# The first two weight units behind two RMS norms, run block by block together

## The chip, the cores and the metric

The kernel runs on one NeuronCore of a Trainium2 chip. The metric is the device time of one execution in microseconds (us). The profile comes from one execution taken by the hardware profiler. TensorE (PE in the rows, PEld its weight loads) multiplies matrices, VectorE (DVE), ScalarE (ACT) and GpSimd (POOL) work elementwise, SyncE (SP) issues most transfers. TensorE's clock has two levels, 1.2 and 2.4 GHz; the rows give the granted clock as a share of full speed, 0.50 or 1.00.

## What is computed

Two transformer blocks on 512 tokens of width 1024, in float32. The first has 16 meta tokens ahead of the sequence, a token mixer (a state space model and an mLSTM) and a gated FFN; the second has a mixed attention and an MLP. Both sublayers of the first block add a normed result, and their sum is normed again for what follows:

```python
def rmsnorm(x, g):
    return x * rsqrt(mean(x * x, -1) + 1e-6) * g
# token_mixer:    x1 = x + rmsnorm(merged @ w_out, g_mix_post)
# channel_mixer:  h = rmsnorm(x1, g_ffn_pre)
#                 y = (gelu(conv3(h @ w_gate)) * (h @ w_up)) @ w_down     (2816 wide)
#                 x2 = x1 + rmsnorm(y, g_ffn_post)
# second block:   q, k, v, ... = rms_norm(x2, attn_norm) @ w_in
```

The change lies at the two places where such a pair of norms stands: x1 to the FFN, and x2 to the second block's projections.

## The kernel before

Activations lie transposed, features in the 128 partitions and tokens along the free axis, as eight tiles (KT = 8) of 128 features. Weights come in 227 units of 128 x 1024 float32, in a ring of four buffers. A unit is one tile of 128 output features: eight blocks of 128 x 128, one for each tile of the input. Every operand is split in a high and a low part of a faster type, and each block takes three products, high by high, low by high and high by low. ScalarE makes w_hi (`split_hi`, L348) and VectorE w_lo (`split_lo`, L848), each two units ahead (LOOK = 2).

On TensorE `unit` (L1689) issues the 24 products of a unit (48 where the output is 516 columns, in two halves of 258), `begin` (L1706) waits first for the unit's w_lo and for the evacuation of the unit before the last, whose PSUM banks it takes over. Each engine works through its own list in a fixed order, and semaphores tie the lists together.

**The stretch around a post norm.** The sublayer's last units leave y_sum. Its squares are summed over the features by products with a matrix of ones (`column_sums`, L1723, plain float32). `rstd` (L868) makes rs of the sums: a scaling on VectorE, a reciprocal root on ScalarE, three Newton steps on VectorE. Then VectorE's `residual` (L1218) goes through the eight tiles: scale y_sum by rs, add it to x (`x1_ready` or `x2_ready`), and, once ScalarE has made h_hi of the tile, make h_lo (`h2_lo` or `h3_lo`). ScalarE also squares the tile (`tile_square`, L369) for the next norm. TensorE does not wait for the next norm's rs: the units run on x times the gain alone, and rs is multiplied in when a unit is evacuated. So the first unit behind the norm (`ffn_gate` of U_FFN, or `wide(U_V2, ...)`) waits block by block for h_lo, and behind each block stands `tile_sum` (L1733), the column sums of that tile's squares. When all eight are through (`stat_mm`), VectorE's second `rstd` makes the new rs, and the first unit is evacuated with it (gate_pad, or v2T), then the second. The third unit needs the first one's banks.

Behind the first norm a gate unit (516 columns, banks 0 and 1 or 2 and 3) and an up unit (512 columns) alternate, and GpSimd convolves the gate's result. Behind the second norm come eight units of values (`wide`, 512 columns, banks 0 and 1 in turn). Each is evacuated to v2T, turned by four transposes on TensorE (`v2_transposes`, L1991, banks 2 and 3 in turn) and copied by ScalarE (`v2_copy`, L654), in a list where the copy of unit n - 1 stands in front of the split of unit n + 3.

Of the kernel before, what the change touches and what calls it, by code (L numbers as in the profile page):

```python
# [23 lines left out]
P = 128  # L24
D_MODEL = 1024
KT = D_MODEL // P
SEQ, META = 512, 16
T1 = SEQ + META
HALF = T1 // 2
T0 = 12  # L30
TW = T1 - T0
# [14 lines left out]
RING = 4  # L46
# [18 lines left out]
U_FFN = U_OUT + KT  # L65
FFN_CHUNKS = (8, 8, 6)
U_V2 = U_FFN + 2 * FFN_TILES + 3 * KT
U_F2 = U_V2 + KT
U_G0 = U_F2 + 1
U_QK2 = U_G0 + 1  # L70
# [74 lines left out]
def build(nc, w_units, x_t, cols_in, consts_in, sel_in, ssm_b_in, ssm_c_in, alibi_in, dil_in, out):  # L145
# [6 lines left out]
    def fixed(name, shape, dt=fp32):  # L152
        t = nc.alloc_sbuf_tensor_at(name, [P] + shape, dt, offset=place[0])
        place[0] += (4 * math.prod(shape) + 31) // 32 * 32
        return t
# [10 lines left out]
    whi = fixed("w_hi", [RING, 1024], f32r)  # L166
    wlo = fixed("w_lo", [RING, 1024], f32r)
    tile528 = KT * T1 * 4
    Zx = region(tile528)
    hhi = fixed("h_hi", [KT, T1], f32r)  # L170
    hlo = fixed("h_lo", [KT, T1], f32r)
# [86 lines left out]
    PS = nc.alloc_psum_tensor("ps", [P, 8, 512], fp32)  # L258
# [3 lines left out]
    def sem(name):  # L262
        if name not in sems:
            sems[name] = nc.alloc_semaphore(name)
        return sems[name]
# [3 lines left out]
    unit_done, evacuated = sem("unit_done"), sem("evacuated")  # L269
# [38 lines left out]
    with block as block:  # L308
# [1377 lines left out]
        def _(pe):  # L1686
            mm = nc.tensor.matmul

            def unit(s, r, xhi, xlo, outs, ready=None, base=0, blocks=None, last_of_unit=True, after=None):  # L1689


                blocks = blocks or [(k, k) for k in range(KT)]
                for b, (kw, kx) in enumerate(blocks):
                    if ready is not None:
                        pe.wait_ge(ready, base + kx + 1)
                    w = slice(kw * P, kw * P + P)
                    for a, (wt, xt) in enumerate(((whi, xhi), (whi, xlo), (wlo, xhi))):
                        for o, c0, n in outs:
                            ins = mm(o, wt[:, s % RING, w], xt[:, kx, c0:c0 + n], start=(b == 0 and a == 0),  # L1699
                                     stop=(b == len(blocks) - 1 and a == 2))  # L1700
                    if last_of_unit and b == len(blocks) - 1:
                        ins.then_inc(unit_done, 1)
                    if after is not None:
                        after(b)

            def begin(s, r=0):  # L1706
                pe.wait_ge(lo_ready, r + (s + 1))
                if s >= 2:
                    pe.wait_ge(evacuated, r + (s - 1))
# [5 lines left out]
            def late_halves(s, b0=None, c0=T0):  # L1715
                b = 2 * (s % 2) if b0 is None else b0
                return [(PS[:, b + h, 0:TH], c0 + TH * h, TH) for h in range(2)]

            def column_sums(n, src, start, stop):

                outs = [(4, 0, n // 2), (5, n // 2, n // 2)] if n != SEQ else [(4, 0, SEQ)]
                for b, c0, k in outs:
                    ins = mm(PS[:, b, 0:k], ones, src[:, c0:c0 + k], start=start, stop=stop)  # L1723
                return ins
# [8 lines left out]
            def tile_sum(norm, n, m):  # L1733

                pe.wait_ge(sem("tile_sq"), KT * PRE.index(norm) + m + 1)
                column_sums(n, sqm[m] if norm == 5 else sq[m % 2], m == 0, m == KT - 1).then_inc(sem("tile_summed" if m < KT - 1 else "stat_mm"), 1)
# [156 lines left out]
            for n in range(U_GLU):  # L1893
                begin(n)
                if n == 0:
                    unit(n, 0, hhi, hlo, halves(n), sem("h1_lo"), after=lambda b: tile_sum(0, T1, b))
                else:
                    unit(n, 0, hhi, hlo, halves(n) if n < U_O else late_halves(n))
                if 1 <= n <= CT:
                    turn_tokens(n - 1)  # L1900
                if n in B_AFTER:
                    b_transposes(B_AFTER.index(n))
                if n == GATE_AFTER:
                    gate_transposes()
                if n == K_AFTER:
                    ssm_kernel()
                if n in Y_AFTER:
                    ssm_out(Y_AFTER.index(n))
                if n in E_AFTER:
                    ssm_in(E_AFTER.index(n))  # L1910
                if n in VT_AFTER:
                    v_transposes(VT_AFTER.index(n))
                if n >= U_GA - 1:
                    h, k = divmod(n - (U_GA - 1), 4)
                    if h < HEADS1:
                        (mlstm_broadcast, mlstm_scores, mlstm_values, mlstm_norm)[k](h)
# [5 lines left out]
            for n in range(U_GLU, U_MERGE):  # L1922
                begin(n)
                unit(n, 0, yahi, yalo, late_halves(n), None, 0, [(k, k) for k in range(4)], False)
                unit(n, 0, yahi, yalo, late_halves(n, 4 + 2 * (n % 2)), None, 0, [(4 + k, k) for k in range(4)])
# [9 lines left out]
            for s in (U_MERGE, U_MERGE + 1):  # L1935
                begin(s)
                branch(s, 1)
# [18 lines left out]

            def ffn_gate(s, r):
                begin(s, r)
                if isinstance(r, int) and s == U_FFN:
                    unit(s, r, hhi, hlo, late_halves(s, c0=0), sem("h2_lo"), after=lambda b: tile_sum(2, TW, b))  # L1960
                else:
                    unit(s, r, hhi, hlo, late_halves(s, c0=0))

            def ffn_up(s, r):
                begin(s, r)
                unit(s, r, hhi, hlo, [(PS[:, 2 * (s % 2), :], META - T0, SEQ)])

            def down(s, r, xhi, xlo, o, ready=None, base=0, tiles=KT):
                begin(s, r)
                unit(s, r, xhi, xlo, [(o, 0, SEQ)], ready, base, [(k, k) for k in range(tiles)])  # L1970

            s0, f0 = U_FFN, 0
            for c, tiles in enumerate(FFN_CHUNKS):
                for q in range(2):
                    ffn_gate(s0 + 2 * q, 0)
                    ffn_up(s0 + 2 * q + 1, 0)
                with pe.Fori(0, tiles // 2 - 1) as i:
                    for q in range(2, 4):
                        ffn_gate(s0 + 2 * q, i * 4)
                        ffn_up(s0 + 2 * q + 1, i * 4)  # L1980
                s0 += 2 * tiles
                with pe.Fori(0, 2) as i:
                    for j in range(4):
                        down(s0 + j, i * 4, fahi, falo, PS[:, 2 * ((s0 + j) % 2), :], sem("fa_lo") if j == 0 else None,
                             f0, tiles)
                f0 += tiles
                s0 += KT
# [3 lines left out]
            def v2_transposes(j):  # L1991
                pe.wait_ge(evacuated, U_V2 + j + 1)
                if j >= 2:
                    pe.wait_ge(sem("v2_ready"), j - 1)
                for t in range(4):
                    ins = nc.tensor.transpose(PS[:, 2 + j % 2, P * t:P * t + P], vT2[j % 2][:, P * t:P * t + P], ident)
                ins.then_inc(sem("v2t_mm"), 1)

            def wide(s, r=0, ready=None, norm=None):
                begin(s, r)  # L2000
                unit(s, r, hhi, hlo, [(PS[:, s % 2, :], 0, SEQ)], ready,
                     after=(lambda b: tile_sum(norm, SEQ, b)) if norm else None)

            pe.wait_ge(evacuated, U_V2)
            wide(U_V2, 0, sem("h3_lo"), 4)
            for n in range(U_V2 + 1, U_QK2):
                wide(n)
                if n <= U_F2:
                    v2_transposes(n - 1 - U_V2)

# [140 lines left out]
            for j in range(KT // 2):  # L2151
                s = U_OB + j
# [8 lines left out]
            for m in range(KT):  # L2161
                s = U_MLP + KT + m
                down(s, 0, mahi, malo, PS[:, s % 2, :], sem("ma_lo") if m == 0 else None, 0)
            with pe.Fori(0, 2) as c:
                for f in range(KT):
                    wide(U_MLP + 2 * KT + f, c * 16)
                for m in range(KT):
                    s = U_MLP + 3 * KT + m
# [3 lines left out]
            for m in range(KT):  # L2172
                s = U_MLP + 7 * KT + m
# [124 lines left out]
```

## Time and profile before

| | |
|---|---|
| median of 3 runs | 1564.51 us (1563.32 to 1565.14) |
| the profiled execution | 1565.74 us |
| its span, first to last instruction | 1563.9 us |
| busy: TensorE / its weight loads | 1496.9 us (96%) / 1290.1 us (82%) |
| busy: VectorE / ScalarE / GpSimd | 844.1 us (54%) / 616.3 us (39%) / 267.0 us (17%) |
| mean granted clock of TensorE | 0.986 |
| chain that ended last | TensorE 85%, VectorE 7%, GpSimd 4%, ScalarE 2%, issue 2% |

A busy TensorE need not be at its full rate: products are pipelined and the end of a record is modelled. The pitch from one record's start to the next is what a product costs in a row of them. The two stretches that the change touches are at about 442 to 490 us (first post norm) and 838 to 890 us (second).

### The profile page before, as it was taken

The numbers are of one execution on the slowest core, as the hardware profiler recorded it, in microseconds if no ns is written. First come the engines' busy times: TensorE is split into PE (matmuls) and PEld (weight loads), VectorE is DVE, ScalarE is ACT, GpSimd is POOL, SyncE is SP. The second block draws the span as 40 slices with busy tenths as digits, with TensorE's granted clock in tenths as the row PEclk, the third lists the DMA queues.
The fourth block names the chain that finished last, engine by engine and source line by source line (L and its number), as shares of the span: only waits on it lengthen the run. The fifth ranks groups of instructions, "written<-read, shape, count | busy, mean of one in ns | idle before, by whom it ended". The sixth has DMA issues, their size and how long they took to land.

```text
span 1563.9 us, 23462 instructions
## 1 busy us (share of the span) xinstructions
PE 1496.9 (96%) x9229; PEld 1290.1 (82%) x9229; DVE 844.1 (54%) x1227; ACT 616.3 (39%) x920; POOL 267.0 (17%) x272
## 2 busy tenths in 40 slices
PE   7978999999979999999997999999999999999998
PEld 7977999999968988988885777888886888888887
DVE  5779744357465543553455546776845533434344
ACT  5547655643243221231233334646534323223230
POOL 2664100000025613540632000000100000000000
PEclk9989999999999999999998999999999999999999
DMA  5211211123302222222232221111122222223221
GB/s 191 83 42 54 69 54 56 67 82 137 108 28 95 94 94 94 91 97 95 81 108 74 73 76 55 43 39 55 41 81 95 91 97 95 95 94 95 92 95 67
DMA packets 36006, 128.03 MB, mean 82 GB/s; under 512 B 4460, under 2 KB 4588, under 8 KB 35792
## 3 DMA queue, kind: packets, MB, share of 16 engines
q1 hardware_dynamic: 34464, 122.18, 23.3%
q10 hardware_dynamic: 864, 4.33, 0.7%
q8 instruction: 63, 1.03, 0.3%
q0 software_dynamic: 592, 0.30, 0.1%
q14 instruction: 23, 0.19, 0.0%
HBM read 124.68 MB, written 2.10 MB: 81 GB/s over the span
## 4 chain that ended last, share of the span: by engine, by line
PE 85%; DVE 7%; POOL 4%; ACT 2%; issue 2%; DMA 0%; SPq 0%; DVEq 0%; POOLq 0%; ACTq 0%
PE ps L1699 72%; PE ps L2036 2%; PE ps L2060 2%; PE ps L1881 1%; PE ps L1723 1%; POOL phase_tmp L1568 1%; PE ps L2047 1%; PE ps L1831 1%; DVE h_lo L866 1%; DVE w_lo L853 1%; PE ps L2014 1%; DVE x L866 1%; POOL acc L1568 1%; POOL phase L1568 1%; POOL conv_tmp L1657 1%
## 5 line engine op out<-in xcount | busy, mean ns | idle before, releaser
L1699 PE MATMUL ps<-h_hi,w_hi 128*128 128x258 f32 (+2 forms) x1768 | 512.3, 339 | 38.9 <-DVE h_lo L866 18.2
L1699 PE MATMUL ps<-h_lo,w_hi 128*128 128x258 f32 (+2 forms) x1768 | 494.3, 329 | 0.0
L1699 PE MATMUL ps<-h_hi,w_lo 128*128 128x258 f32 (+2 forms) x1768 | 493.2, 328 | 0.0
L853 DVE TENSOR_TENSOR w_lo<-w_raw,w_hi 128x1024 fp32r<-128x1024 f32 (+2 forms) x227 | 290.5, 1280 | 182.6 <-ACT w_hi L355 181.4
L1699 PEld LDWEIGHTS ps<-h_hi,w_hi 128*128 128x128 f32 x1768 | 301.9, 190 | 90.1 <-issue 34.8
L1699 PEld LDWEIGHTS ps<-h_lo,w_hi 128*128 128x128 f32 x1768 | 299.5, 190 | 33.8 <-issue 5.9
L1699 PEld LDWEIGHTS ps<-h_hi,w_lo 128*128 128x128 f32 x1768 | 299.5, 190 | 30.8
L355 ACT ACTIVATE w_hi<-w_raw 128x1024 fp32r<-128x1024 f32 (+2 forms) x227 | 233.2, 1035 | 199.6 <-PE ps L1699 198.6
L1699 PE MATMUL ps<-mlp_lo,w_hi 128*128 128x512 f32 x256 | 100.9, 394 | 0.0
L1699 PE MATMUL ps<-mlp_hi,w_hi 128*128 128x512 f32 x256 | 100.3, 392 | 0.0
L1699 PE MATMUL ps<-mlp_hi,w_lo 128*128 128x512 f32 x256 | 99.4, 388 | 0.0
L857 DVE TENSOR_TENSOR y_sum<-y_sum,ps 128x512 f32<-128x512 f32 (+1 forms) x40 | 27.5, 688 | 112.9 <-PE ps L1699 112.9
L1699 PE MATMUL ps<-ffn_hi,w_hi 128*128 128x512 f32 x176 | 68.7, 391 | 2.1 <-DVE ffn_lo L857 2.1
L1699 PE MATMUL ps<-ffn_hi,w_lo 128*128 128x512 f32 x176 | 69.3, 394 | 0.0
L1699 PE MATMUL ps<-ffn_lo,w_hi 128*128 128x512 f32 x176 | 68.9, 392 | 0.0
L1654 POOL TENSOR_SCALAR gate_conv<-gate_pad,cols 128x512 f32<-128x512 f32 x22 | 29.2, 1326 | 212.8 <-DVE gate_pad L857 212.8
L818 ACT ACTIVATE relu<-ps 128x512 f32<-128x512 f32 x32 | 19.2, 601 | 105.3 <-PE ps L1699 105.3
L626 ACT ACTIVATE gate_conv<-gate_conv 128x512 f32<-128x512 f32 x22 | 13.9, 632 | 117.3 <-POOL gate_conv L1568 117.3
L866 DVE SCALAR_TENSOR_TENSOR relu_sq<-ps,relu 128x512 f32<-128x512 f32 x32 | 22.1, 692 | 70.1 <-ACT relu L818 70.1
L1568 POOL TENSOR_TENSOR gate_conv<-gate_conv,conv_tmp 128x512 f32<-128x512 f32 x44 | 56.8, 1292 | 3.7
L1657 POOL TENSOR_SCALAR conv_tmp<-gate_pad,cols 128x512 f32<-128x512 f32 x44 | 56.7, 1289 | 4.2
L1699 PEld LDWEIGHTS ps<-mlp_hi,w_hi 128*128 128x128 f32 x256 | 48.1, 188 | 11.2
(292 smaller groups left out, 1936.3 us busy)
## 6 DMA issues: line engine op xcount, KB each, us to landing
w_raw<-w_units SPq DMA_DIRECT2D x227, 512.0 KB, 3.3
x<-x_t ACTq DMA_DIRECT2D x1, 2112.0 KB, 7.8
out<-out_tile SPq DMA_DIRECT2D x8, 256.0 KB, 2.0
x<-x_t ACTq DMA_DIRECT2D x3, 528.0 KB, 9.2
x<-x_t ACTq DMA_DIRECT2D x2, 264.0 KB, 4.7
consts<-consts SPq DMA_DIRECT2D x1, 320.0 KB, 6.9
b_step<-ssm_b SPq DMA_DIRECT2D x1, 256.0 KB, 10.4
c_step<-ssm_c SPq DMA_DIRECT2D x1, 256.0 KB, 11.3
```

Of the source, the lines that this page charges most:

```text
L355: A.do(dn.activation(whi[:, s % RING, 0:w], raw[:, s % RING, 0:w], ACT.Copy), hi_ready)
L818: A.do(dn.activation(rl[p][:, :], PS[:, s % 2, :], ACT.Relu), sem("relu_ready"))
L853: Dv.do(v.tensor_tensor(wlo[:, s % RING, 0:w], raw[:, s % RING, 0:w], f32(whi[:, s % RING, 0:w]), ALU.subtract), lo_ready)
L857: Dv.do(v.tensor_tensor(o, a, b, op), s)
L866: Dv.do(v.scalar_tensor_tensor(out=o, in0=a, scalar=sc, in1=b, op0=op0, op1=op1), s)
L1568: Po.do(g.tensor_tensor(o, a, b, op), s)
L1654: Po.do(g.tensor_scalar(dst[:, :], src[:, META:META + SEQ], w[0], w[3], M, A_))
L1657: Po.do(g.tensor_scalar(ctmp[:, :], src[:, META + k:META + k + SEQ], w[k], 0.0, M, A_))
L1699: ins = mm(o, wt[:, s % RING, w], xt[:, kx, c0:c0 + n], start=(b == 0 and a == 0), stop=(b == len(blocks) - 1 and a == 2))
L1723: ins = mm(PS[:, b, 0:k], ones, src[:, c0:c0 + k], start=start, stop=stop)
L2036: ins = mm(PS[:, b + bank, c:c + w], q[0:65, hh, P * t:P * t + P], k[0:65, hh, 0:w], start=False, stop=True, skip_group_check=True)
L2060: ins = mm(PS[:, 2 + 3 * hh, HD * t:HD * t + HD], Pb[hh][:, bank, c + P * k:c + P * k + P], V[:, k, HD * h:HD * h + HD], start=(k == 0), s ...
```

## The change

A new helper, `two_units`, runs two units over the same input together: it waits for block k of h_lo, issues block k of the first unit, then the column sums of tile k, then block k of the second unit (with `lag` = 0, as both calls have it). Behind the first post norm the pair is the first gate and the first up unit; behind the second it is the first two value units. The second unit's own `begin` moves between the first unit's first block and its own. The first value unit's transposes, which stood behind the second unit, now stand behind the third, directly ahead of the second unit's. Which products are computed does not change, nor does any other engine's list.

```diff
--- before.py
+++ after.py
@@ -1703,6 +1703,31 @@
                     if after is not None:
                         after(b)
 
+            def block_of(s, xhi, xlo, outs, k):
+
+                for a, (wt, xt) in enumerate(((whi, xhi), (whi, xlo), (wlo, xhi))):
+                    for o, c0, n in outs:
+                        ins = mm(o, wt[:, s % RING, k * P:k * P + P], xt[:, k, c0:c0 + n], start=(k == 0 and a == 0),
+                                 stop=(k == KT - 1 and a == 2))
+                return ins
+
+            def two_units(s, outs, ready, base, lag, after):
+
+                begin(s)
+                for k in range(KT + lag):
+                    if k < KT:
+                        pe.wait_ge(ready, base + k + 1)
+                        ins = block_of(s, hhi, hlo, outs[0], k)
+                        if k == KT - 1:
+                            ins.then_inc(unit_done, 1)
+                        after(k)
+                    if k == lag:
+                        begin(s + 1)
+                    if k >= lag:
+                        ins = block_of(s + 1, hhi, hlo, outs[1], k - lag)
+                        if k - lag == KT - 1:
+                            ins.then_inc(unit_done, 1)
+
             def begin(s, r=0):
                 pe.wait_ge(lo_ready, r + (s + 1))
                 if s >= 2:
@@ -1956,10 +1981,7 @@
 
             def ffn_gate(s, r):
                 begin(s, r)
-                if isinstance(r, int) and s == U_FFN:
-                    unit(s, r, hhi, hlo, late_halves(s, c0=0), sem("h2_lo"), after=lambda b: tile_sum(2, TW, b))
-                else:
-                    unit(s, r, hhi, hlo, late_halves(s, c0=0))
+                unit(s, r, hhi, hlo, late_halves(s, c0=0))
 
             def ffn_up(s, r):
                 begin(s, r)
@@ -1972,6 +1994,10 @@
             s0, f0 = U_FFN, 0
             for c, tiles in enumerate(FFN_CHUNKS):
                 for q in range(2):
+                    if s0 + 2 * q == U_FFN:
+                        two_units(U_FFN, (late_halves(U_FFN, c0=0), [(PS[:, 2 * ((U_FFN + 1) % 2), :], META - T0, SEQ)]), sem("h2_lo"), 0, 0,
+                                  lambda k: tile_sum(2, TW, k))
+                        continue
                     ffn_gate(s0 + 2 * q, 0)
                     ffn_up(s0 + 2 * q + 1, 0)
                 with pe.Fori(0, tiles // 2 - 1) as i:
@@ -2002,9 +2028,12 @@
                      after=(lambda b: tile_sum(norm, SEQ, b)) if norm else None)
 
             pe.wait_ge(evacuated, U_V2)
-            wide(U_V2, 0, sem("h3_lo"), 4)
-            for n in range(U_V2 + 1, U_QK2):
+            two_units(U_V2, [[(PS[:, (U_V2 + j) % 2, :], 0, SEQ)] for j in range(2)], sem("h3_lo"), 0, 0,
+                      lambda k: tile_sum(4, SEQ, k))
+            for n in range(U_V2 + 2, U_QK2):
                 wide(n)
+                if n == U_V2 + 2:
+                    v2_transposes(0)
                 if n <= U_F2:
                     v2_transposes(n - 1 - U_V2)
 
```

## Rows read from the trace of the kernel before

**Rows 1.** Page, chain that ended last; list of waits (total, times, longest).

```profile
PE 85%; DVE 7%; POOL 4%; ACT 2%; issue 2%; DMA 0%; SPq 0%; DVEq 0%; POOLq 0%; ACTq 0%
...
PE ps L1699 <- DVE h_lo L866: 18.2, 12, 6.9
```

**Rows 2.** Timeline, VectorE, first norm: start us, us, engine, line, operation.

```profile
465.20 0.76 DVE L866 SCALAR_TENSOR_TENSOR h_lo<-x,cols,h_hi 128x516 fp32r<-128x516 f32 x1 [0.18 <-ACT h_hi L608]
...
467.54 0.75 DVE L866 SCALAR_TENSOR_TENSOR h_lo<-x,cols,h_hi 128x516 fp32r<-128x516 f32 x1 [0.79 <-ACT h_hi L608]
...
469.01 1.23 DVE L853 TENSOR_TENSOR w_lo<-w_raw,w_hi 128x1024 fp32r<-128x1024 f32 x1 [0.72 <-ACT w_hi L355]
...
470.35 0.70 DVE L863 TENSOR_SCALAR rs<-ps 128x516 f32<-128x516 f32 x1
...
473.93 0.69 DVE L857 TENSOR_TENSOR gate_pad<-ps,rs 128x516 f32<-128x516 f32 x1
```

**Rows 3.** Timeline, TensorE, first norm.

```profile
452.04 0.77 PE L1699 MATMUL ps<-h_hi,w_hi 128*128 128x258 f32 x2 [6.86 <-DVE h_lo L866]
...
453.47 1.92 PE L1723 MATMUL ps<-sq,consts 128*128 128x258 f32 x4
...
468.35 0.51 PE L1699 MATMUL ps<-h_hi,w_hi 128*128 128x258 f32 x2 [0.48 <-DVE h_lo L866]
...
469.17 1.03 PE L1723 MATMUL ps<-sq,consts 128*128 128x258 f32 x4
...
469.85 0.58 PE L1699 MATMUL ps<-h_hi,w_hi 128*128 128x512 f32 x1
...
475.61 0.40 PE L1699 MATMUL ps<-h_hi,w_hi 128*128 128x258 f32 x2
```

**Rows 4.** Timeline, VectorE and TensorE, second norm.

```profile
852.38 0.77 PE L1699 MATMUL ps<-h_hi,w_hi 128*128 128x512 f32 x1 [6.77 <-DVE h_lo L866]
...
865.46 0.75 DVE L866 SCALAR_TENSOR_TENSOR h_lo<-x,cols,h_hi 128x512 fp32r<-128x512 f32 x1 [0.19 <-ACT h_hi L650]
...
867.79 0.75 DVE L866 SCALAR_TENSOR_TENSOR h_lo<-x,cols,h_hi 128x512 fp32r<-128x512 f32 x1 [0.79 <-ACT h_hi L650]
...
868.59 0.50 PE L1699 MATMUL ps<-h_hi,w_hi 128*128 128x512 f32 x1 [0.50 <-DVE h_lo L866]
...
869.39 1.02 PE L1723 MATMUL ps<-sq,consts 128*128 128x512 f32 x2
...
870.58 0.69 DVE L863 TENSOR_SCALAR rs<-ps 128x512 f32<-128x512 f32 x1
...
874.15 0.69 DVE L857 TENSOR_TENSOR v2T<-ps,rs 128x512 f32<-128x512 f32 x1
...
875.82 0.60 PE L1996 MATMUL ps<-consts,v2T 128*128 128x128 f32 x4
...
876.17 0.48 PE L1699 MATMUL ps<-h_hi,w_hi 128*128 128x512 f32 x1
```

**Rows 5.** Timeline, VectorE and TensorE, what follows behind each norm.

```profile
483.54 0.69 DVE L857 TENSOR_TENSOR gate_pad<-ps,rs 128x516 f32<-128x516 f32 x1
...
487.00 0.40 PE L1699 MATMUL ps<-h_hi,w_hi 128*128 128x258 f32 x2
...
878.03 1.23 DVE L853 TENSOR_TENSOR w_lo<-w_raw,w_hi 128x1024 fp32r<-128x1024 f32 x1 [1.32 <-ACT w_hi L355]
```

**Rows 6.** Windows: stretch, us, busy of five engines, granted clock, DMA share, GB/s.

```profile
124.85:128.70 3.85, 0.00 (x0) 0.00 (x0) 3.75 (x9) 3.69 (x6) 1.29 (x2) 1.00 0.00 0
...
128.70:136.70 8.00, 7.95 (x124) 7.78 (x125) 7.86 (x16) 5.87 (x8) 2.88 (x3) 0.79 0.07 22
...
452.00:460.00 8.00, 7.96 (x37) 7.24 (x38) 7.32 (x11) 3.99 (x7) 0.00 (x0) 0.71 0.01 2
...
852.00:860.00 8.00, 7.35 (x18) 4.37 (x19) 7.29 (x12) 3.73 (x6) 0.00 (x0) 0.75 0.00 0
...
929.50:936.50 7.00, 5.76 (x25) 4.54 (x25) 3.22 (x5) 1.58 (x2) 0.00 (x0) 1.00 0.20 74
```

## The prediction

> **What bounds the kernel now.** I read the chain's shares and the list of waits first [rows 1]. The chain that ended last is 85% TensorE: nearly everywhere the time is the number of matmuls times their pitch, so a change of order can only win where TensorE stands still or runs slowly. The wait for h_lo is the largest entry of TensorE's list, 18.2 us, and much of it lies behind the two post norms. There the profiled timeline shows the same picture twice. VectorE makes one block of the new h_lo every 2.34 us behind the first norm [rows 2] and every 2.33 us behind the second [rows 4], and TensorE has, for each block, only the products of the first unit and the column sums. After the eighth block comes the second unit, all at once, and beside it the chain that the third unit needs: scale the sums into rs, reciprocal root on ScalarE, three Newton steps, then the evacuation of the first unit. That chain starts at 470.35 and its evacuation ends at 473.93 + 0.69 = 474.62, which is 4.27 us [rows 2]; behind the second norm it runs from 870.58 to 874.15 + 0.69 = 874.84, 4.26 us [rows 4]. Today the second unit (5.6 us) covers it: the third unit starts without a wait, at 475.61 and at about 876.26 [rows 3, 4]. So the question is whether TensorE has room for the second unit's products between the blocks, and what covers the rs chain once the second unit is gone from behind it.
>
> **The prices, at full clock.** One block of the first FFN unit, six products of 258 columns, starts at 468.35 + 0.51 - 0.40 = 468.46 (a first record is longer by the time it waits at the array) and the sums start at 469.17: 0.71 us [rows 3]. The sums: the next unit's first product is recorded at 469.85 for 0.58 us where such a product takes 0.39, so it really streams from 470.04: the sums hold TensorE for 0.87 us. The whole second unit, 24 products of 512 columns, goes from 470.04 to 475.61, 5.57 us, or 0.70 us for the three products of a block [rows 3]. At the low clock I take double the last two; the first is seen: 452.04 + 0.77 - 0.63 = 452.18 to 453.47, 1.29 us [rows 3].
>
> **First norm, does TensorE keep up?** A block now asks of TensorE 0.71 + 0.87 + 0.70 = 2.28 us, against 2.34 us that VectorE gives. There is room, but only 0.06 us a block, and it starts with a debt. TensorE begins this stretch at 1.2 GHz: of 452 to 460 the granted clock is 0.71 on average, which is 0.29 x 2 x 8 = 4.6 us at half speed, until 456.6 [rows 6]. The first block's work takes 1.29 + 1.74 + 1.40 = 4.4 us there; the second starts at 456.6, when its h_lo has long been ready, is then at full clock, and ends at about 458.9. Five more blocks of 2.28 us put the start of the eighth at 470.3, where it is 468.46 today: 1.8 us late. This is worked out, not seen. Its sums end 0.71 + 0.87 + 0.17 us later (0.17 is what the drain adds: 469.17 + 1.03 - 470.04), at 472.05, and rs can begin at 472.1 instead of 470.35, where it waits for about the same time for the weight split in front of it. The evacuation then ends at 474.62 + 1.7 = 476.3, and the third unit streams from 476.45 instead of 475.61: **+0.85 us**. The second unit's seven blocks (4.9 us) did move into the gaps, but 1.8 us of that is lateness and the rest is a new wait: TensorE has finished block eight of both units at 470.3 + 2.3 = 472.6 and stands still until 476.45, **3.9 us**.
>
> **Second norm.** Same sum. Per block 0.70 + 0.87 + 0.70 = 2.27 us at most; the three products here are 0.69 and I use 2.25, against 2.33. Start 852.38 + 0.77 - 0.63 = 852.5 [rows 4]; the low clock lasts to 856.0 (0.25 x 2 x 8 = 4.0 us of 852 to 860) [rows 6], so the first block ends at 856.45, and six more of 2.25 us bring the eighth to 869.95; today it begins 0.16 us behind the end of h_lo at 868.54, so 1.25 us late [rows 4]. Today the sums end at 869.39 + 1.02 = 870.41, later 871.65; rs moves from 870.58 to 871.7, the evacuation ends at 875.95 and the third unit streams from 876.1. Today it streams from 876.17 + 0.48 - 0.39 = 876.26, but with the first transposes already done. These are moved behind it, four of them in 0.45 us (875.82 to 876.26) [rows 4], and must still be paid: **+0.3 us**. Here too the wait is 876.1 - 872.2 = **3.9 us**.
>
> **What the moved transposes stand in front of.** ScalarE's queue is copy, then the split of a later weight unit; the copy of the first transposes now waits for the third unit, and the split behind it with it. Today the split on VectorE ends at 878.03 + 1.23 = 879.26, 3.0 us behind the transposes [rows 5]; add an evacuation of 0.69 us, and 3.7 us have to fit beside the second transposes and the fourth unit, 0.45 + 5.57 = 6.0 us. They do: nothing, with 2.3 us in hand. Behind the first norm the whole FFN pipeline on GpSimd, ScalarE and VectorE starts 1.7 us later against a third unit that is 0.85 us later. Its next result TensorE asks for is the evacuation at 483.54 + 0.69 = 484.23, needed at 487.00 [rows 5]: 2.8 us in hand, no cost, and 0.9 us less in hand than today. No DMA is moved, GpSimd's and SP's queues keep their order, and no computation is added or dropped.
>
> **The clock.** What does TensorE do after a wait of 3.9 us? Nearly the same thing is in this trace. From 124.85 to 128.70 it stands still for 3.85 us with the clock at full, and of the next 8 us the granted clock is 0.79: 0.21 x 2 x 8 = 3.4 us at 1.2 GHz, with TensorE busy throughout [rows 6]. Two other waits, of 3.6 and of 3.1 us, have this same average behind them. A wait of 1.2 us, at 929.8 to 931.0, leaves the clock at 1.00 [rows 6]. The new waits are as long as the longest of these, so I expect the drop at both. Each costs half of 3.4 us, 1.7 us of work, **+3.4 us** for both; seen from the two stretches behind the norms it can be up to 4.6 us at the low clock (2.3 us each), and from the 1.2 us wait nothing. I take the middle value, since its wait is as long. The Trainium skill says, in TensorE: Matmul & The Clock Gate, "What's actually happening", that "the default state is throttled, and activity releases the throttle", and in "HAM oscillation — how this bites in real kernels" that every stall long enough starts the next burst cold, each time anew. That speaks against this change: the matmuls gathered into the gaps are paid back behind a stall. The rows agree for 3.85 us. With that rule the sum is +4.5 us, without it +1.1 us.
>
> **The sum.** 0.85 + 0.3 + 3.4 = 4.5 us. The profiled execution took 1565.74 us (span 1563.9 and 1.8 around it) and would take 1570.2. It lies 1.2 us above the median of the runs, 1564.51, which becomes 1569.0.
>
> **Rivals.** *The clock stays up* at one or both waits, since the wait is shared between two stretches of activity: +1.1 to +2.8 us, 1565.6 to 1567.3. For it speaks only the 1.2 us wait; against it the three long ones. Chance 0.18. *TensorE keeps pace* and the clock drops: if the first block costs less at the low clock than I make it, or blocks are done faster than 2.28 us, rs starts as today and the third units begin at 474.75 (-0.85 us) and 874.97 plus the transposes (-0.85 us); with the drops -1.7 + 3.4 = +1.7 us, 1566.2. Chance 0.10. *The other side:* it keeps pace and no drop comes: -1.7 us, 1562.8. It hangs on one thing, a block's work on TensorE against VectorE's 2.34 us: once the debt at block two is under 0.4 us (six blocks of 0.06) it is gone by block eight. Chance 0.05. More than this can't be won, since the rs chain of 4.3 us bounds the start of the third unit; over 3.1 us faster would need a gain that I don't see, 0.03. *More low stretches* than two, or a low clock over two such stretches, since all later work is shifted: 1571 or more, 0.04. The forecast itself, late blocks and two drops, has 0.60, and its own range is 1567.0 to 1571.0: the drops cost 1.5 to 2.3 us each, and a later rise of the clock in the first blocks adds its half to the lateness.
>
> **How the numbers follow.** A measurement here tells about 0.2%, 3.1 us, from no change. Slower by more: of the 0.60 some 0.52, with the last rival and the top of the first 0.60. Faster by more: 0.04. Within: 0.36. The range 1564.0 to 1571.2 leaves out the case of the other side, the unexplained gain, and most of the last, some 0.15.
>
> **What would show it.** In the changed profile, first norm: three products of 512 columns between the sums and the next block; the eighth block 1 to 2 us behind its h_lo; a wait of TensorE for gate_pad (behind the second norm for v2T) of 3.5 to 4 us; the granted clock at 0.5 for about 3.4 us behind each. The step on pace is wrong if the eighth block starts with its h_lo; the step on the clock if the third units run at the 0.23 us pitch from the first product. The forecast falls if the rs chain is no longer what the third unit waits for.

## The result and the profile after

| | before | changed |
|---|---|---|
| median | 1564.58 us | 1567.85 us (8 runs, 1566.34 to 1570.98) |
| profiled execution / its span | 1565.74 / 1563.9 us | 1566.34 / 1564.5 us |
| waits of TensorE for h_lo, gate_pad, v2T | 18.2, none, none us | 14.0, 3.8, 3.7 us |

The ratio of the runs is 1.0022, 95% interval 1.0013 to 1.0031: the change costs 3.3 us. The profiled execution is the fastest of the eight, 1.5 us under their median, while that of before lies 1.2 us over its own; so the two profiles are only 0.6 us apart. The page of the changed kernel (span; busy; chain that ended last):

```profile
span 1564.5 us, 23462 instructions
...
PE 1494.7 (96%) x9229; PEld 1291.7 (83%) x9229; DVE 843.4 (54%) x1227; ACT 616.6 (39%) x920; POOL 266.7 (17%) x272
...
PE 86%; DVE 6%; POOL 4%; ACT 2%; issue 1%; DMA 0%; SPq 0%; DVEq 0%; POOLq 0%; ACTq 0%
```

The list of TensorE's waits (total, times, longest). L1710 is the product in the new helper:

```profile
PE ps L1710 <- DVE h_lo L866: 13.6, 2, 6.9
...
PE ps L1699 <- DVE gate_pad L857: 3.8, 1, 3.8
...
PE ps L1699 <- DVE v2T L857: 3.7, 1, 3.7
...
PE ps L1748 <- POOL acc L1568: 3.6, 2, 3.3
```

Against [rows 1], TensorE waits less for h_lo (13.6 us and 0.4 on another line, after 18.2), and two waits are new, one for the evacuation of the first unit behind each norm.

Timeline of TensorE and VectorE, first norm, changed kernel (start, us, engine, line, operation; the lines that answer to [rows 2, 3]):

```profile
451.57 0.77 PE L1710 MATMUL ps<-h_hi,w_hi 128*128 128x258 f32 x2 [6.86 <-DVE h_lo L866]
...
470.14 0.40 PE L1710 MATMUL ps<-h_hi,w_hi 128*128 128x258 f32 x2
...
470.86 1.03 PE L1748 MATMUL ps<-sq,consts 128*128 128x258 f32 x4
...
471.93 0.70 DVE L863 TENSOR_SCALAR rs<-ps 128x516 f32<-128x516 f32 x1 [1.74 <-PE ps L1748]
...
475.52 0.69 DVE L857 TENSOR_TENSOR gate_pad<-ps,rs 128x516 f32<-128x516 f32 x1
...
476.36 0.48 PE L1699 MATMUL ps<-h_hi,w_hi 128*128 128x258 f32 x2 [3.77 <-DVE gate_pad L857]
...
478.22 0.63 PE L1699 MATMUL ps<-h_hi,w_hi 128*128 128x258 f32 x2
...
483.72 0.40 PE L1699 MATMUL ps<-h_hi,w_hi 128*128 128x512 f32 x1
```

Count from the first product. In the kernel before the eighth block streamed from 468.46, 16.4 us after it; now from 470.14, 18.6 us after: 2.15 us late. rs begins 20.36 us after it instead of 18.31, and the third unit streams from 476.44, 24.87 instead of 23.57 us: 1.3 us late although it follows a wait of 3.8 us. From 477.4 to 480.8 its pairs of products (258 columns each) come every 0.43 us instead of 0.24, and the whole unit lasts to 483.72, 7.3 us for 5.8.

The same behind the second norm ([rows 4]):

```profile
853.16 0.77 PE L1710 MATMUL ps<-h_hi,w_hi 128*128 128x512 f32 x1 [6.77 <-DVE h_lo L866]
...
870.46 0.39 PE L1710 MATMUL ps<-h_hi,w_hi 128*128 128x512 f32 x1
...
872.21 0.69 DVE L863 TENSOR_SCALAR rs<-ps 128x512 f32<-128x512 f32 x1 [0.93 <-PE ps L1748]
...
875.77 0.69 DVE L857 TENSOR_TENSOR v2T<-ps,rs 128x512 f32<-128x512 f32 x1
...
876.61 0.62 PE L1699 MATMUL ps<-h_hi,w_hi 128*128 128x512 f32 x1 [3.74 <-DVE v2T L857]
...
883.82 1.04 PE L2022 MATMUL ps<-consts,v2T 128*128 128x128 f32 x8
...
884.61 0.47 PE L1699 MATMUL ps<-h_hi,w_hi 128*128 128x512 f32 x1
```

The eighth block is 0.98 us late (17.30 us after the first product; 16.32 before) and rs 0.85 us (19.05, 18.20 before). The third unit streams from 876.60, 23.44 us after it, where it was 23.88 with four transposes done ahead of it; these now stand behind the third unit (the eight of 883.82) and take their 0.45 us there. That is even, but for the clock. Windows of the changed kernel (stretch, us, busy of the five engines, granted clock, DMA share, GB/s):

```profile
472.60:476.30 3.70, 0.00 (x0) 0.00 (x0) 2.90 (x6) 2.86 (x3) 0.00 (x0) 1.00 0.12 49
476.30:484.30 8.00, 7.94 (x51) 7.88 (x52) 1.98 (x3) 1.58 (x2) 5.63 (x5) 0.79 0.20 68
872.80:876.60 3.80, 0.07 (x1) 0.02 (x1) 3.00 (x6) 1.58 (x2) 0.00 (x0) 1.00 0.32 124
876.60:884.60 8.00, 7.99 (x32) 6.47 (x33) 1.59 (x2) 0.14 (x1) 0.00 (x0) 0.79 0.19 68
```

Both waits run out at full clock, and of the 8 us behind each the granted clock is 0.79, 3.4 us at half speed, as in [rows 6]. The low stretch does not begin at the same point: 1.0 us into the third unit behind the first norm, and with its first product behind the second (876.61, 877.03, 877.46: a pitch of 0.43 us).

**Where the 3.3 us lie.** I divided every profile at four marks: A from the first h_lo product of the first norm to the column sums of the second post norm, P from there to the second norm's first product, B on to the scan of the forget gates (a single operation on VectorE over 512 columns), R the rest. What stands ahead of A is the same code in all of these kernels except e5 to e7 and e12, which have idle products there. In the others' profiles it took 451.1 to 452.8 us (452.0 before, 451.6 changed): that much moves without any change. Besides [rows 3, 4] the marks of the kernel before and of the changed one are:

```profile
842.07 1.84 PE L1723 MATMUL ps<-acc,consts 128*128 128x512 f32 x2 [3.31 <-POOL acc L1568]
...
924.46 1.21 DVE L1308 TENSOR_TENSOR_SCAN fox<-consts,fox 6x512 f32<-6x512 f32 x1
```

```profile
844.40 1.13 PE L1748 MATMUL ps<-acc,consts 128*128 128x512 f32 x2 [3.30 <-POOL acc L1568]
...
926.87 1.21 DVE L1308 TENSOR_TENSOR_SCAN fox<-consts,fox 6x512 f32<-6x512 f32 x1
```

| kernel | A | P | B | R | median, against before in the same comparison |
|---|---|---|---|---|---|
| before | 390.03 | 10.31 | 72.08 | 639.44 | |
| changed | 392.83 | 8.76 | 73.71 | 637.63 | 1567.85, +3.3 |
| e1_first | 392.50 | 9.30 | 72.10 | 638.22 | 1565.62, +0.6 |
| e2_second | 390.05 | 10.43 | 73.87 | 637.68 | 1565.53, +0.5 |
| e3_filled | 391.33 | 10.35 | 72.20 | 639.12 | 1567.37, +2.4 |
| e4_lag5 | 389.29 | 9.64 | 71.30 | 638.03 | 1562.32, -2.7 |
| e5_preheat | 391.68 | 8.75 | 72.91 | 638.23 | 1566.24, +1.6 |
| e6_preheat_filled | 389.28 | 8.75 | 71.33 | 639.57 | 1563.09, -1.6 |
| e7_before_preheat | 390.01 | 10.35 | 72.12 | 639.44 | 1565.13, +0.5 |
| e8_lag3 | 389.33 | 8.76 | 72.93 | 638.01 | 1562.66, -2.0 |
| e9_before_steady | 390.01 | 8.75 | 72.10 | 638.01 | 1562.55, -2.2 |
| e10_after_steady | 392.50 | 8.75 | 75.91 | 637.91 | 1567.84, +3.1 |
| e11_lag5_steady | 389.23 | 8.75 | 71.32 | 639.48 | 1562.44, -2.3 |
| e12_lag5_all | 389.23 | 8.75 | 71.33 | 637.95 | 1563.31, -1.4 |

A and B hold the change: +2.80 and +1.63 us, 4.4 together. P and R hold nothing that it touches, and got 1.55 and 1.8 us shorter in this profile. Two windows in each kernel show most of it; first before, then changed:

```profile
842.00:846.00 4.00, 3.55 (x4) 0.97 (x4) 0.35 (x1) 0.00 (x0) 0.72 (x2) 0.57 0.17 66
938.00:950.00 12.00, 10.09 (x34) 7.45 (x35) 7.51 (x10) 8.08 (x10) 0.00 (x0) 0.86 0.14 45
```

```profile
844.30:846.50 2.20, 1.98 (x4) 0.68 (x4) 0.08 (x1) 0.00 (x0) 0.75 (x2) 1.00 0.33 86
938.00:950.00 12.00, 9.73 (x38) 6.66 (x37) 7.36 (x11) 7.91 (x9) 0.00 (x0) 1.00 0.27 89
```

Before, the column sums of the second post norm and the first projections of the second block each fall into 3.4 us at the low clock (0.43 x 2 x 4, 0.14 x 2 x 12). In the changed kernel's profile both run at full clock. What is done there is the same; it is done 2.3 us later. That the delay decides is an argument and no more. The three profiles with the first norm as before and nothing held off there (before, e2_second, e7_before_preheat) all lose time in P. But e8_lag3 comes to these column sums at 842.10 us, the kernel before at 842.07, and only the latter loses time there (P 8.76 and 10.31); and e3_filled comes to them at 843.43, e5_preheat at 843.41, with 10.35 and 8.75.

### The profile page after: what moved, and what is told of

The parts are those of the page before. It is cut to its first block, busy times and chain, and to the rows that moved or that the text cites. A ratio compares the mean times of both kernels' runs of the same rounds, so it can differ in the third digit from the quotient of the medians.

```text
span 1564.5 us, 23462 instructions
## 1 busy us (share of the span) xinstructions
PE 1494.7 (96%) x9229; PEld 1291.7 (83%) x9229; DVE 843.4 (54%) x1227; ACT 616.6 (39%) x920; POOL 266.7 (17%) x272
## 4 chain that ended last, share of the span: by engine, by line
PE 86%; DVE 6%; POOL 4%; ACT 2%; issue 1%; DMA 0%; SPq 0%; DVEq 0%; POOLq 0%; ACTq 0%
PE ps L1699 71%; PE ps L2065 2%; PE ps L2089 2%; PE ps L1748 2%; PE ps L1710 2%; PE ps L1906 1%; POOL phase_tmp L1568 1%; PE ps L2076 1%; PE ps L1856 1%; DVE w_lo L853 1%; PE ps L2043 1%; POOL acc L1568 1%; POOL conv_tmp L1657 1%; POOL phase L1568 1%; POOL gate_conv L1568 0%
## 5 line engine op out<-in xcount | busy, mean ns | idle before, releaser
L1699 PE MATMUL ps<-h_hi,w_hi 128*128 128x258 f32 (+2 forms) x1728 | 495.2, 336 | 28.1 <-DVE qk L857 8.7
L1699 PE MATMUL ps<-h_lo,w_hi 128*128 128x258 f32 (+2 forms) x1728 | 481.1, 328 | 0.0
L1699 PE MATMUL ps<-h_hi,w_lo 128*128 128x258 f32 (+2 forms) x1728 | 480.1, 328 | 0.0
L1699 PEld LDWEIGHTS ps<-h_hi,w_hi 128*128 128x128 f32 x1728 | 294.0, 190 | 70.3 <-issue 27.5
L1699 PEld LDWEIGHTS ps<-h_lo,w_hi 128*128 128x128 f32 x1728 | 291.8, 190 | 32.2 <-issue 5.0
L1699 PEld LDWEIGHTS ps<-h_hi,w_lo 128*128 128x128 f32 x1728 | 292.3, 190 | 29.7
```

## The experiments

The theory: at each norm the interleaved blocks fall behind from the low clock at the start (the debt), the third unit has to wait for the rs chain that the second unit used to cover, and the clock falls behind that wait. Its rivals are that the clock doesn't count, that the interleaving is slow in itself, and that the loss sits in shifted stretches elsewhere.

**One place at a time.** e1_first takes the changed kernel and gives the second norm its old order:

```diff
-            two_units(U_V2, [[...] for j in range(2)], sem("h3_lo"), 0, 0, ...)
-            for n in range(U_V2 + 2, U_QK2):
+            wide(U_V2, 0, sem("h3_lo"), 4)
+            for n in range(U_V2 + 1, U_QK2):
                 wide(n)
-                if n == U_V2 + 2:
-                    v2_transposes(0)
```

> Only the first post norm has its two units together, the second is as in the kernel before. My theory is that each place pays three things: blocks that run late (a debt from the low clock), a new wait of TensorE for the first unit's evacuation, and a stretch of 3.4 us at 1.2 GHz behind that wait. For this place alone it expects 0.85 + 1.7 = +2.6 us against the kernel before, about 1567.2 us, a wait for gate_pad of 3.8 us, and no wait for v2T. The rival that the clock doesn't count expects +0.9 us, 1565.5. The rival that the loss of the changed kernel comes from stretches that are merely shifted elsewhere expects the part between the first norm and the end of the first FFN chunk to take no longer than before.

e2_second takes the first norm's pair out instead:

```diff
-                    if s0 + 2 * q == U_FFN:
-                        two_units(U_FFN, ...)
-                        continue
```

> Only the second post norm has its two units together (with the moved transposes), the first is as before. The theory expects 0.3 + 1.7 = +2.0 us, about 1566.6 us, a wait for v2T of 3.8 us and 3.4 us at the low clock behind it. Without a part for the clock: +0.3 us, 1564.9.

In its own stretch each cost what was expected: A +2.47 us (2.6) in the one, B +1.79 (2.0) in the other, and the untouched stretch stayed within 0.02 us. The medians didn't follow: +0.6 and +0.5 us, ratio 1.0006 in both, intervals 0.9997 to 1.0016 and 0.9997 to 1.0015. In both profiles the low clock at the first projections is gone (R 638.2 and 637.7), and in e1_first 1.0 of the 1.55 us at the column sums too. So the costs are local, and something gives part of them back elsewhere. The rival without the clock fits the medians and not A and B.

**The clock in the new waits.** Four products that compute nothing of use in each wait (e3_filled):

```diff
+            def fill(n):
+                for _ in range(n):
+                    mm(PS[:, 6, :], ident, consts[:, 0:4, :]..., start=True, stop=True)
...
                         two_units(U_FFN, ...)
+                        fill(4)
...
             two_units(U_V2, ...)
+            fill(4)
```

> The changed kernel, and in each of the two new waits TensorE works on four idle products (the identity by 512 columns of constants in float32, 0.87 us each at full clock, 3.5 us in all, into a PSUM bank that nobody reads). They compute nothing that is used. If the low clock is what the waits cost beyond their length, the third units start when they do in the changed kernel, then run at full clock, and the time falls by 3.4 us against the changed kernel, to about 1564.5, which is 0 to +1.3 us against the kernel before. If the clock doesn't count, or if such products don't hold it, the time stays at 1567.9 (or grows, if the products end after the evacuation).

Its waits (total, times, longest), the idle products behind the first norm, and the window of its third unit:

```profile
PE ps L1699 <- DVE gate_pad L857: 0.3, 1, 0.3
...
PE ps L1699 <- DVE v2T L857: 0.3, 1, 0.3
...
473.01 3.60 PE L1747 MATMUL ps<-consts 128*128 128x512 f32 x8
...
476.50:484.50 8.00, 7.66 (x57) 7.28 (x57) 2.02 (x3) 1.58 (x2) 5.61 (x5) 1.00 0.20 68
```

The idle products end in time (0.3 us of wait are left), the third unit runs at full clock, and A and B fall by 1.50 and 1.51 us against the changed kernel. This is what the clock costs, 3.0 us, and the 1.30 and 0.12 us that remain over before are lateness and the uncovered chain. The median doesn't show it: +2.4 us over before for +3.3, ratio 1.0018 (1.0009 to 1.0027), an interval that overlaps the changed kernel's. This kernel's profile has both low stretches of P and R again.

**The order of the second unit.** The helper's own parameter, both calls:

```diff
-                two_units(..., sem("h2_lo"), 0, 0, ...)
+                two_units(..., sem("h2_lo"), 0, 5, ...)
```

> The changed kernel with lag = 5 at both places: the second unit runs five blocks behind the first, so that three of its blocks stand between the first unit's last ones and five behind them. The theory: the debt of the low clock is paid off before the second unit begins, so rs starts when it does in the kernel before, and six blocks of 0.70 us (4.2 us) behind the last sums cover the rs chain of 4.3 us. No wait, no drop of the clock, each third unit 0.85 us earlier than before: -1.7 us, about 1562.9 us. If interleaving two units costs in itself (weights, banks), it is 1564.6 or more. If it is the moved transposes that cost, +0.5 us.

```profile
PE ps L1699 <- DVE gate_pad L857: 0.4, 1, 0.4
...
PE ps L1699 <- DVE v2T L857: 0.4, 1, 0.4
...
476.00:484.00 8.00, 8.00 (x54) 7.37 (x54) 1.98 (x3) 1.58 (x2) 4.28 (x5) 1.00 0.19 68
...
876.00:884.00 8.00, 8.00 (x41) 6.58 (x40) 2.66 (x3) 2.98 (x4) 0.00 (x0) 1.00 0.17 57
```

No wait to speak of, full clock in the 8 us behind each norm, A and B 0.74 and 0.78 us shorter than before (0.85 each worked out). The median is 2.7 us below before, ratio 0.9984 (0.9975 to 0.9993), and 5.5 us below the changed kernel's. The moved transposes, which are in this kernel too, cost nothing beyond their own products. Here only part of the second unit is interleaved; for all of it e6_preheat_filled, below, shows the same.

With lag = 3 (the same edit) a shorter wait is left:

> The changed kernel with lag = 3: three blocks less of the second unit among the first unit's, four behind the last sums (2.8 us), so the new wait is 3.8 - 3 x 0.70 = 1.7 us. The debt still goes. If a wait of 1.7 us leaves the clock up, both stretches are as with lag = 5 (389.29 and 71.30 us there). If the clock drops behind it too, each is 1.5 us longer, 390.8 and 72.8.

First products of the two third units, with the wait before them, and the 8 us behind each:

```profile
475.57 0.48 PE L1699 MATMUL ps<-h_hi,w_hi 128*128 128x258 f32 x2 [1.68 <-DVE gate_pad L857]
...
873.50 0.47 PE L1699 MATMUL ps<-h_hi,w_hi 128*128 128x512 f32 x1 [1.78 <-DVE v2T L857]
...
475.70:483.70 8.00, 8.00 (x58) 7.59 (x59) 1.98 (x3) 1.59 (x2) 5.47 (x5) 1.00 0.21 68
...
874.60:882.60 8.00, 8.00 (x34) 6.48 (x33) 0.49 (x1) 1.23 (x2) 0.00 (x0) 0.79 0.22 68
```

Both outcomes came, one at each norm: behind 1.68 us the clock stayed (A 389.33), behind 1.78 us it fell for 3.4 us (B 72.93, 1.6 us over lag 5). The two waits stand in different surroundings, and this is one execution; what decides between them is not shown. The median is 2.0 us below before, ratio 0.9987 (0.9977 to 0.9997).

**The debt.** Six idle products between the last column sums of each post norm and its first h_lo, in the changed kernel (e5_preheat), with the waits filled as well (e6_preheat_filled), and in the kernel before (e7_before_preheat):

```diff
             post_stat(1, TW)
+            fill(6)
...
             post_stat(3, SEQ)
+            fill(6)
```

> The changed kernel with six idle products (identity by 512 columns of constants, 0.87 us each, results unused) between the last column sums of each post norm and the first h_lo, where TensorE otherwise stands still for 6.9 us. This takes the debt away: the first blocks run at full clock. If the lateness of the eighth block comes from the low clock in the first blocks, it goes (2.1 us late in the changed kernel, then under 0.2), and each third unit starts 0.85 us earlier than in the kernel before; the wait of 3.8 us and its stretch at the low clock stay. From the first h_lo product to the column sums of the second post norm: 390.03 us before, 392.83 changed, 390.7 expected; from the second norm's first h_lo product to the scan of the forget gates: 72.08, 73.71, 72.7 expected. If instead the interleaved blocks are too long in themselves for VectorE's pitch, the lateness stays and so do 392.8 and 73.7.

> The former, and four idle products in each of the new waits. Neither debt nor drop: 389.2 and 71.2 us for the two stretches, each 0.85 us less than in the kernel before; in all -1.7 us and what the clock does elsewhere. If the products in the wait end after the evacuation, up to 0.3 us more at each place.

> The kernel before with the same six idle products ahead of the first h_lo at both norms. There TensorE has the time to catch up anyway, so the two stretches stay at 390.0 and 72.1 us. If they fall, the low clock in the first blocks costs the kernel before something too, and part of what the former run gains isn't the debt of the interleaving.

The changed kernel with them (window of the first blocks, the eighth block, the third unit's first products, and the window from the fall of the clock to its rise):

```profile
451.50:459.50 8.00, 7.77 (x46) 6.71 (x46) 7.28 (x12) 3.83 (x7) 0.00 (x0) 1.00 0.01 2
...
468.11 0.45 PE L1710 MATMUL ps<-h_hi,w_hi 128*128 128x258 f32 x2
...
474.46 0.77 PE L1699 MATMUL ps<-h_hi,w_hi 128*128 128x258 f32 x2 [3.86 <-DVE gate_pad L857]
...
473.40:480.20 6.80, 5.74 (x27) 5.77 (x28) 2.62 (x4) 0.25 (x1) 5.41 (x5) 0.51 0.25 80
```

The first blocks run at full clock, and rs begins 18.3 us after the first product, as it did before: the lateness is gone, so all of it was the low clock's debt. The wait is now 3.9 us and the third unit starts at the low clock. A is 391.68 (390.7 expected): the clock falls near 473.4, before the third unit begins at 474.46, and comes back near 480.2 (granted 0.51 over all of that), so 5.7 us of the unit's work are at half speed where I had counted 3.4. B is 72.91 (72.7). With the waits filled too, 389.28 and 71.33 us, 0.75 us under before each, which is what lag 5 gives. All eight blocks of both units are interleaved there, so interleaving costs nothing in itself. In the kernel before the same products change nothing, 390.01 and 72.12. Ratios: 1.0008 (0.9998 to 1.0017), 0.9988 (0.9979 to 0.9998), 1.0001 (0.9991 to 1.0010).

**What the shift does elsewhere.** Idle products ahead of the column sums of the second post norm and behind the first statistics of the second block:

```diff
+            fill(3)
             post_stat(3, SEQ)
...
             qk_stat(0, 1)
+            fill(2)
```

in the kernel before (e9_before_steady), the changed one (e10_after_steady) and lag 5 (e11_lag5_steady):

> The two places where the profile of the kernel before has a stretch at the low clock and that of the changed kernel has none: the column sums behind the last FFN units (842.3 to 845.7) and the first projections of the second block (941.3 to 944.7). Three idle products before the former and two before the latter hold the clock. This is the kernel before with them. My theory is that the changed kernel's two places cost 4.4 us and that the 1.1 us missing in the medians comes from these two stretches, which the shift moves into or out of TensorE's idle time. Then this kernel loses both: 1.55 + 1.6 us, about 1561.5.

> The changed kernel with the same five idle products. With both stretches gone in either kernel, the difference to the former run is what the change itself costs, 4.4 us by the two profiles: about 1565.9. If the change itself costs only the 3.3 us of the medians, 1564.8.

> lag = 5 with the same five idle products: 1.5 us below the kernel before with them, about 1560.0.

P is 8.75 us in all three, and R falls to 638.0 in the first two. The kernel before gains 2.2 us by it (3.15 expected), ratio 0.9989 (0.9980 to 0.9998). The changed kernel gains nothing against before: 1567.84, and lies 5.3 us over e9_before_steady where I expected 4.4. Lag 5 gains nothing either (1562.44, where I expected 1560.0); its profile has a low stretch that the kernel before has not (granted clock 0.57 from 1163.5 to 1167.5 us), and R is 639.5. In the profile of e10_after_steady, which is the slowest of its eleven runs, the second norm costs more than in any other, B +3.8 us:

```profile
853.00:861.00 8.00, 7.52 (x17) 4.98 (x18) 7.29 (x11) 3.85 (x7) 0.00 (x0) 0.59 0.00 0
876.50:884.50 8.00, 6.18 (x17) 4.92 (x18) 3.34 (x5) 0.00 (x0) 0.00 (x0) 0.57 0.21 66
```

There the first blocks have 5.9 us at the low clock (0.41 x 2 x 8, less the 0.6 ahead of the first product) instead of 3.1 in the changed kernel's profile, so rs is 2.2 us late instead of 0.85, and the third unit has 6.9 us of low clock around it (0.43 x 2 x 8). So the price of the change moves with the clock: 1.6 to 3.8 us for the second norm in three profiles (changed, e2_second, this one). The changed kernel's eight runs spread over 4.6 us where the eight of before spread over 2.0 (and the 33 beside e10_after_steady over 2.9); whether this is why can't be read, since only the profiled runs show the clock by stretches.

**More of the same, a miss.** Idle products in three further waits (e12_lag5_all):

```diff
+                if n in Y_AFTER[:2]:
+                    pe.wait_ge(evacuated, n)
+                    fill(4, 2 * ((n + 1) % 2))
                 if n in Y_AFTER:
                     ssm_out(Y_AFTER.index(n))
...
+            fill(3, 5)
             pe.wait_ge(sem("y2_lo"), KT)
```

> The former, and idle products in three more waits of 3.1 to 3.9 us, each of which has 3.4 us at the low clock behind it in the kernel before: two in the state space model (four products each, into the banks of the next unit, at 124.8 and 152.9) and one ahead of the dilated heads' output (three, at 1177). If each drop costs 1.7 us, 5.1 us less than the former, about 1554.9. Where the products end after the wait does, it is less. It is my proposal for a kernel that beats both.

1563.31 us, ratio 0.9993 (0.9984 to 1.0002), 0.9 us worse than without. Its waits:

```profile
PE ps L1747 <- DVE qk L857: 2.4, 1, 2.4
...
PE ps L1747 <- DVE vT L857: 2.1, 1, 2.1
...
PE ps L1861 <- issue: 1.1, 1, 1.1
...
PE ps L1699 <- DVE y_dil_lo L866: 0.6, 1, 0.6
```

In the state space model the bank that I had taken for free was not: the idle products (L1747) wait 2.4 and 2.1 us for the evacuation. The low clock then falls into them (granted 0.68 over the first four), and each four take 5.4 us for 3.5. They end after the work that they should precede could have begun, and the first norm's first product comes at 455.34 us, 3.5 us later than in e11_lag5_steady. The third place, ahead of the dilated heads' output, did what it should: 0.6 us of its wait of 3.2 are left, the granted clock from 1180 to 1184 us is 1.00 where the kernel before has 0.57, and R is 637.95 after 639.48.

## Why the prediction was right, and where it was off

- *What the places cost.* 4.5 us were worked out, 4.4 us are in A and B. First norm 2.55 predicted, 2.80 measured; second 2.0, measured 1.63.
- *The lateness.* The block's work was 2.29 us (2.28 worked out), the eighth block 2.15 us late (1.8). The term that was too small is the low clock behind the first product: 4.4 us by the profile of before, 5.2 us in the changed one (0.32 x 2 x 8.5 us of 451.5 to 460, less the 0.2 us ahead of the product). In e1_first it was 4.5 us again, and rs came 1.76 us late, as worked out; so this term moves from one execution to the next. Behind the second norm it was 3.1 us for 3.5, and the eighth block 0.98 us late for 1.25. e5_preheat shows that the debt explains all of the lateness.
- *The new wait.* 3.9 us expected, 3.8 and 3.7 found, behind the units that were named.
- *The clock.* It fell behind both waits, for 3.4 us each. Its price was put at half of that, 1.7 us; e3_filled measures 1.5. The pitch of the products goes from 0.24 to 0.43 us, not to twice 0.24, and 3.4 x (1 - 0.24 / 0.43) = 1.5. The Trainium skill's rule (TensorE: Matmul & The Clock Gate, "HAM oscillation — how this bites in real kernels") that a burst behind a long stall starts cold, and does so each time, is borne out as far as a low stretch follows both waits. The burst does not always start cold: behind the first norm its first 1.0 us ran at full clock, and in e5_preheat the clock fell during the wait. The rival by which the clock stays up has fallen for these waits. Behind the shorter waits of lag 3, 1.68 and 1.78 us, both outcomes came.
- *The moved transposes* cost nothing beyond their own 0.45 us, as predicted, and TensorE's waits show no new one behind them.
- *The step that failed* is the one from the places to the whole. I let later low stretches only be added ("more low stretches", 0.04) and not be lost, and put what lies outside the two places at nothing. In the changed profile two that the kernel before has are absent, 1.55 us in P and 1.8 in R, and the median is 3.3 us instead of 4.5 up. Holding them off in both kernels takes 2.2 us (0.3 to 3.1) from the one and nothing measurable from the other, so the direction is shown. Its share in the medians, and what decides whether such a stretch comes, stay open.
- *The rivals "keeps pace"* were wrong in the changed kernel and are what lag 5 and e6_preheat_filled make true. The bound given for that case, -0.85 us for each place, came out as -0.74 and -0.78.

## What to carry to other kernels

Matmuls moved into an engine's idle gaps are only won if nothing leaned on them where they stood: ask what chain they covered, and leave as much behind as covers it (here six of eight blocks, lag = 5, which beats both kernels). A wait of TensorE can cost more than its length: the low clock around waits of 3.7 to 3.9 us cost 1.5 us more in the changed kernel, 2.4 us in e5_preheat (first norm) and some 2.2 us in e10_after_steady (second). Low stretches elsewhere in a kernel come and go by a few microseconds from one profile to the next, so the parts must be measured from mark to mark before the total is believed: here two changes of +2.5 and +1.8 us each showed as +0.6 and +0.5.

## What the runs showed of the hardware

- Idle products held TensorE's clock at 1.00 through waits of 3.7 and 6.9 us and cost nothing while they ended in time (e3_filled, e5_preheat, e7_before_preheat).
- Two waits of nearly one length, 1.68 and 1.78 us, in one profile had different clocks behind them: 1.00 and 0.79 over 8 us (e8_lag3).
- In e5_preheat the clock fell near 473.4 us, 2.8 us into a wait that began at 470.6; in the changed kernel a wait of nearly the same length ran out at 1.00.
- The low clock did not double the time: pairs of products of 258 columns went from a pitch of 0.24 us to 0.43, products of 512 columns from 0.23 to 0.43.
- The same kernel's runs spread over 2.0 us before and 4.6 us changed (eight each), those of e4_lag5 over 1.1 us and those of e11_lag5_steady, with the same blocks at the norms, over 3.3 us. What sets the spread stays open.
